# A decoder trunk on eight cores: the depthwise convolution as dense matmuls over four time phases, fewer expert weights cast ahead, token numbers scattered and rows gathered

## What is computed

```
u = xn @ w_pw1 + b_pw1                      # 1024 -> 2048
u = a * sigmoid(g)                          # a, g: halves of u
u = depthwise causal conv, width 31, over positions, + b_dw
u = silu(layer_norm(u, ln_g, ln_b)) @ w_pw2 + b_pw2
...
for e in range(16):                         # 2 nonzero weights per token
    y += combine[:, e] * ((silu(xf @ w_gate[e]) * (xf @ w_up[e])) @ w_down[e])
```

## Time and profile before

| what | us |
|---|---|
| median of 3 runs (2652.67 to 2663.49) | 2657.18 |
| the profiled execution | 2669.73 |
| its span, slowest core (core 2; the others from 2623.5) | 2668.7 |
| PE busy (share of the span) | 1926.4 (72%) |
| DVE, ACT, POOL busy | 882.5, 826.5, 391.1 |
| casts and other POOL-queue DMAs, share of 16 engines | 44.3% |
| SP-queue DMAs, share of 16 engines | 25.4% |

### The profile page before, as it was taken

The page is one execution under the profiler, slowest core; times in us unless marked ns, Lnnn a source line. Parts: engine busy times, 40 slices in busy tenths (PEclk is TensorE's granted clock), DMA queues, the critical chain, the costliest instruction groups (busy, mean ns, idle before and its releaser), DMA issues.

```text
span 2668.7 us, 35704 instructions; the slowest of 8 cores (2623.5 to 2668.7 us)
## 1 busy us (share of the span) xinstructions
PE 1926.4 (72%) x11760; PEld 1058.9 (40%) x11760; DVE 882.5 (33%) x1838; ACT 826.5 (31%) x1322; POOL 391.1 (15%) x469
## 2 busy tenths in 40 slices
PE   4999993770439998256777877777993389995557
PEld 1344440220125555122245655555631155553223
DVE  2321102440433332244443333333234423321433
ACT  2411115310112222133545555555511122221333
POOL 0010003201120001332300000010102300012243
PEclk9999995785669999566878999989996689997577
DMA  9999999999039998722235677788741169997333
GB/s 234 186 130 155 135 141 142 129 144 180 32 116 305 322 316 291 175 78 71 33 33 82 99 101 107 107 96 114 104 165 40 75 213 317 326 322 198 125 130 119
DMA packets 126134, 412.93 MB, mean 155 GB/s; under 512 B 34912, under 2 KB 34912, under 8 KB 101360
## 3 DMA queue, kind: packets, MB, share of 16 engines
q0 software_dynamic: 64544, 189.35, 44.3%
q1 hardware_dynamic: 60816, 220.07, 25.4%
q10 hardware_dynamic: 576, 1.05, 0.2%
HBM read 428.58 MB, written 205.78 MB: 238 GB/s over the span
## 4 chain that ended last, share of the span: by engine, by line
PE 63%; DVE 10%; DMA 9%; issue 7%; ACT 6%; another core or an unknown queue 2%; POOL 1%; DVEq 0%; ACTq 0%; SPq 0%; POOLq 0%
PE ps L256 59%; PE ps L260 5%; DMA xt<-xsd 3%; DMA gb<-ysd,slots 2%; ACT sq L273 2%; DMA h<-xT 2%; DMA ring<-w 1%; DVE gb L294 1%; DVE xnb L294 1%; ACT pt L273 1%; DVE q L294 1%; ACT rt L273 1%; DMA xsd<-xrow,slots 1%; ACT rstd L273 1%
## 5 line engine op out<-in xcount | busy, mean ns | idle before, releaser
L256 PE MATMUL ps<-xTT,ring 128*128 128x384 bf16 (+1 forms) x2304 | 355.4, 315 | 2.4 <-DVE xTT L300 2.0
L256 PE MATMUL ps<-sq,ones_bf 128*128 128x512 bf16 x288 | 140.3, 502 | 230.1 <-ACT sq L273 228.0
L256 PEld LDWEIGHTS ps<-xTT,ring 128*128 128x128 bf16 x2304 | 215.6, 98 | 141.1 <-issue 6.0
L256 PE MATMUL ps<-glu,dg 128*128 128x512 bf16 x992 | 216.9, 381 | 6.2 <-DVE dg L276 6.2
L256 PE MATMUL ps<-xgD,wh 128*128 128x512 bf16 x512 | 150.8, 447 | 84.7 <-DVE q L294 56.0
L273 ACT ACTIVATE pt<-ps,cst_s 128x512 bf16<-128x512 f32 (+1 forms) x288 | 180.6, 658 | 89.4 <-PE ps L256 83.0
L260 PE MATMUL ps<-cst_s,gb 128*128 128x128 f32 x256 | 62.1, 424 | 191.8 <-DVE gb L294 177.9
L273 ACT ACTIVATE sq<-h 128x512 bf16<-128x512 f32 x192 | 113.3, 623 | 219.3 <-PE ps L256 147.2
L256 PE MATMUL ps<-ring,hdn 128*128 128x512 bf16 x800 | 180.9, 382 | 0.5 <-DVE hdn L276 0.4
L256 PEld LDWEIGHTS ps<-sq,ones_bf 128*128 128x128 bf16 x288 | 29.7, 103 | 376.9 <-issue 372.8
L256 PE MATMUL ps<-xgA,w 128*128 128x512 bf16 x768 | 172.3, 388 | 3.6 <-DVE h L294 3.6
(11 more groups left out here) (184 smaller groups left out, 2590.4 us busy)
## 6 DMA issues: line engine op xcount, KB each, us to landing
w<-w_moe POOLq DMA_DIRECT2D x96, 1024.0 KB
ring<-w SPq DMA_DIRECT2D x96, 1024.0 KB
ysd<-ysb SPq DMA_DIRECT2D x96, 512.0 KB
xt<-xsd SPq DMA_DIRECT2D x32, 768.0 KB
xsd<-zt SPq DMA_DIRECT2D x16, 1024.0 KB
ysd<-zt SPq DMA_DIRECT2D x9, 1024.0 KB
yT<-h SPq DMA_DIRECT2D x32, 256.0 KB
h<-xT SPq DMA_DIRECT2D x28, 256.0 KB
```

Source lines behind the costliest of these rows:

```text
L256: return self.op('pe', lambda e: e.matmul(out, lhsT=lhsT, rhs=rhs, start=start, stop=stop, **kw), ins=[lhsT, rhs], outs=[out], inc=inc)
```

## The change

Four things. (1) The convolution. Channels are taken in 32 groups of 32, and a partition becomes (time modulo 4, channel in the group), so that a column holds four neighbouring tokens. The 31 taps become 9 shifts v of dense 128x128 matrices (4 x 4 phases, diagonal in the channel), each applied to the 512 columns that hold all 2048 tokens: 32 x 9 = 288 matmuls. DVE builds 36 such matrices for 4 groups in one operation (`build`). The layout is reached through DRAM: the gated output `gp` (3 buffers) is written to `gpd` by 4 DMAs and read back into `gc` by one (`regroup`), on SP, in runs of 512 bfloat16, for each chunk of 128 channels; after normalisation and Silu each chunk goes back the same way (one write on SP, 4 reads, two on ACT's queue). The first pointwise matmul now runs chunk by chunk over all tokens, its weights in four buffers of one chunk, read in runs of 128 columns; the convolution of chunk c-2 follows that of chunk c, and the sums for the layer norm run in between over two fixed PSUM banks. (2) Of layer 0 only 9 experts are cast ahead (27 casts, one after each unit of `pw1` from the second chunk on). The others, 0, 1, 2, 5, 8, 11 and 14, are loaded from float32 into `ring` on POOL's queue, and the spare experts of layer 0 fetch float32 rows. (3) Rows of x are written once, by SP, to `xnd`; only the token numbers are scattered, 4 bytes each, to `idxd`; `xi` reads them back and `load_x` gathers the rows on POOL's queue, three indirect DMAs for an expert, in both layers. `back` gets 17 more small DVE operations for these addresses. (4) `xsd` and its zeroing are gone; the 19 zeroing DMAs of `ysd`, 512 KB each, are issued on SP in layer 0's `back`.

```diff
+NA = CAP // 128
+IX1 = 16 * CAP
+NIDX = IX1 + 16 * 128 + 128
+PRE0 = tuple(e for e in range(3, 16) if e not in (5, 8, 11, 14))
...
+def pack_conv(inp):
+    wdw = np.asarray(inp['conv_w_dw'][0], dtype=np.float32).reshape(31, 32, 32)
+    wsh = np.zeros((4, 32, 32, 9, 4), dtype=np.float32)
+    for i in range(4):
+        for v in range(9):
+            for j in range(4):
+                k = 4 * v + i - j - 2
+                if 0 <= k <= 30:
+                    wsh[i, :, :, v, j] = wdw[k].T
...
-                S.dma('act' if tt0 == 0 and c % 2 else 'sp', h[:, c, tt0 * TT:(tt0 + 1) * TT],
-                      xv[:, c, tt0 * TT:(tt0 + 1) * TT])
-        casts = [(l, e, j) for l in range(2) for e in range(NE) for j in range(3)]
+                x_tok = S.dma('act' if tt0 == 0 and c % 2 else 'sp', h[:, c, tt0 * TT:(tt0 + 1) * TT],
+                              xv[:, c, tt0 * TT:(tt0 + 1) * TT])
+            x_toks.append(x_tok)
+        casts = [(l, e, j) for l in range(2) for e in (range(NE) if l else PRE0) for j in range(3)]
...
+
+                load_w1(0)
+                load_w1(1)
+                S.dma('act', cva[:], cva_d)
+                S.wait_tok('pool', x_toks[2])
+                load_w1(2)
+                S.wait_tok('pool', x_toks[3])
+                load_w1(3)
+                S.memset('pool', gc[:, :, 0:8], 0.0)
+                S.copy('dve', blk[:], cva[:, NG * 36:NG * 36 + 128])
+                m32 = cva[:, NG * 36 + 128:NG * 36 + 256].rearrange("p (j c) -> p j c", c=32)
+                S.memset('dve', zi[:], 0)
+                S.dma('act', idxd.rearrange("(p a) o -> p (a o)", p=128), zi[:], outs=[("idx", 0, 1, 0, 100)])
+
+                def build(c):
+                    S.tt('dve', dg[:, c % 2], m32.unsqueeze(1).to_broadcast([128, 36, 4, 32]),
+                         cva[:, c * 144:(c + 1) * 144].rearrange("p (a j) -> p a j", j=4).unsqueeze(3).to_broadcast([128, 36, 4, 32]),
+                         ALU.mult)
+
+                P1, P2 = PS[6], PS[7]
+                ps_set[0] = list(range(6))
+                done = [0]
+
+                def pw1(c, tt):
+                    pa = next_ps()
+                    pg = next_ps()
+                    for k in range(NC8):
+                        S.mm(pa[:], w1[:, c % 4, 0, k, :], xn(k, tt * TT, TT), k == 0, k == NC8 - 1)
+                    for k in range(NC8):
+                        S.mm(pg[:], w1[:, c % 4, 1, k, :], xn(k, tt * TT, TT), k == 0, k == NC8 - 1)
+                    S.act(sg[:, tt % 2, :], pg[:], AF.Sigmoid, bias=P('b_pw1', 8 + c))
+                    S.stt(gp[:, c % 3, :, tt * 128:(tt + 1) * 128].rearrange("p i u -> p u i"),
+                          pa[:].rearrange("p (u i) -> p u i", i=4), P('b_pw1', c),
+                          sg[:, tt % 2, :].rearrange("p (u i) -> p u i", i=4), ALU.add, ALU.mult)
+                    if c > 0 and len(casts) > NE * 3:
+                        pump(1)
+
+                def regroup(c):
+                    for gg in range(4):
+                        S.dma('sp', gpd[4 * c + gg].rearrange("i c u -> c i u"), gp[32 * gg:32 * gg + 32, c % 3],
+                              outs=[("gpd", 0, 1, 4 * c + gg, 4 * c + gg + 1)])
+                    S.dma('sp', gc[:, 4 * c:4 * c + 4, 8:GW], gpd[4 * c:4 * c + 4].rearrange("g i c u -> (i c) g u"),
+                          ins=[("gpd", 0, 1, 4 * c, 4 * c + 4)])
+                    if c + 4 < NC8:
+                        load_w1(c + 4)
+
+                def stats(g):
+                    S.mm(P1[:], blk[:], gc[:, g, 8:GW], g == 0, g == NG - 1)
+                    S.mm(P2[:], blk[:], sq[:, g % 2, :], g == 0, g == NG - 1)
+
+                def conv(c):
+                    for gg in range(4):
+                        g = 4 * c + gg
+                        ps = next_ps()
+                        for v in range(9):
+                            S.mm(ps[:], dg[:, c % 2, gg * 9 + v].rearrange("p j c -> p (j c)"), gc[:, g, v:v + TT],
+                                 v == 0, v == 8)
+                        S.act(gc[:, g, 8:GW], ps[:], AF.Identity, bias=P('b_dwP', g))
+                        S.act(sq[:, g % 2, :], gc[:, g, 8:GW], AF.Square)
+                        if g:
+                            stats(g - 1)
+
+                for tt in range(NTT):
+                    rms_tile(tt, 'g_mix', 0, lambda k, t1=tt: xn(k, t1 * TT, TT))
+                    for c in range(2):
+                        pw1(c, tt)
...
+                build(0)
+                regroup(0)
+                regroup(1)
+                for c in range(2, NC8 + 2):
+                    if c < NC8:
+                        for tt in range(NTT):
+                            pw1(c, tt)
+                        regroup(c)
+                    if c - 1 < NC8:
+                        build(c - 1)
+                    conv(c - 2)
+                stats(NG - 1)
+                p2.close()
                 w2 = sb("w2", [128, NC8, D], BF16, pc)
                 w2v = w_pw2.rearrange("(c p) n -> p c n", p=128)
                 for c in range(NC8):
                     S.dma('pool', w2[:, c, :], w2v[:, c, :])
-
-                def cvb(c, tt):
-                    return xn(c, tt * TT, TT)
...
                 mean = sb("meanA", [128, TT], F32, pc)
-                m2 = sb("m2A", [128, TT], F32, pc)
...
+                for g in range(NG):
+                    v = gc[:, g, 8:GW]
+                    S.tt('dve' if g % 5 in (1, 3) else 'pool', t1[:, g % 3, :], v, mean[:], ALU.subtract)
+                    S.tt('dve', t2[:, g % 3, :], t1[:, g % 3, :], rstd[:], ALU.mult)
+                    S.act(v, t2[:, g % 3, :], AF.Silu, bias=P('ln_bP', g), scale=P('ln_gP', g))
+                    c, gg = g // 4, g % 4
+                    if gg == 3:
+                        S.dma('sp', gpd[4 * c:4 * c + 4].rearrange("g i c u -> (i c) g u"), gc[:, 4 * c:4 * c + 4, 8:GW],
+                              outs=[("gpd", 0, 1, 4 * c, 4 * c + 4)])
+                        for q in range(4):
+                            S.dma('sp' if q % 2 else 'act', xg[0][32 * q:32 * q + 32, c, :].rearrange("p (i u) -> p i u", i=4),
+                                  gpd[4 * c + q].rearrange("i c u -> c i u"),
+                                  ins=[("gpd", 0, 1, 4 * c + q, 4 * c + q + 1)])
...
                 def load_w(e):
                     for j in range(3):
-                        S.dma('sp', ring[:, e % NBR, j * NIN:(j + 1) * NIN], w16[l][e, :, j * NIN:(j + 1) * NIN],
-                              ins=[("w16", 0, 1, (l * NE + e) * 3 + j, (l * NE + e) * 3 + j + 1)])
+                        if l or e in PRE0:
+                            S.dma('sp', ring[:, e % NBR, j * NIN:(j + 1) * NIN], w16[l][e, :, j * NIN:(j + 1) * NIN],
+                                  ins=[("w16", 0, 1, (l * NE + e) * 3 + j, (l * NE + e) * 3 + j + 1)])
+                        else:
+                            S.dma('pool', ring[:, e % NBR, j * NIN:(j + 1) * NIN].rearrange("p (a n) -> p a n", n=2048),
+                                  w_moe[l, e, :, j * NIN:(j + 1) * NIN].rearrange("p (a n) -> p a n", n=2048))
 
...
+                    S.copy('dve', pf[:], sf[:])
...
                     S.tt('dve', ov2[:], ov2[:], ok2[:], ALU.mult)
@@ -794,6 +885,24 @@
                     S.ts('dve', sf[:], sf[:], dump[:], ALU.add, 0.0, ALU.max)
...
+                    S.ts('dve', isl[:, tt % 2], ri[:], float(NIDX - 1), ALU.min)
+                    zero(5)
...
-                            S.dma('pool', xsd, xrow[:, i % 3, :], out_idx=slots[:, i, k:k + 1], ins=[("xsdz", 0, 1, 0, 100)],
-                                  outs=[("xsd", 0, 1, 2 * i + k, 2 * i + k + 1)])
+                            S.dma('pool', idxd, tokid[:, i:i + 1], out_idx=isl[:, tt % 2, i4, k:k + 1],
+                                  ins=[("idx", 0, 1, 50, 51)], outs=[("idx", 0, 1, 2 * i + k, 2 * i + k + 1)])
...
+                S.dma('sp', xi[:], idxd[0:IX1, :].rearrange("(p a) o -> p (a o)", p=128), ins=[("idx", 0, 1, 0, 51)])
...
+                for q in range(NSP):
+                    S.dma('pool', xs[:, q:q + 1], idxd, in_idx=ov0[:, 0, q:q + 1], ins=[("idx", 0, 1, 0, 51)])
...
                 def load_x(e):
-                    if e < NE:
-                        S.dma('sp', xt[:, e % 2, 0:CAP // 128], xsd[e * CAP:(e + 1) * CAP, :].rearrange("(a p) d -> p a d", p=128),
-                              ins=[("xsd", 0, 1, 0, 64)])
-                    else:
-                        S.dma('pool', xt[:, e % 2, 0, :], xsd, in_idx=ov0[:, 0, e - NE:e - NE + 1],
-                              ins=[("xsd", 0, 1, 0, 64)])
+                    for a in range(tiles_of[e]):
+                        S.dma('pool', xt[:, e % 2, a, :], xnd,
+                              in_idx=xi[:, e * NA + a:e * NA + a + 1] if e < NE else xs[:, e - NE:e - NE + 1],
+                              ins=[("xnd", 0, 1, 0, 16)])
```

183 lines of the change are left out of this document (91 added, 92 removed).

## The result

The changed kernel takes **2804.69 us** (median of 4 runs, 2768.11 to 2883.61), the kernel before 2659.66 beside it (2652.67 to 2663.49): ratio **1.0478**, 95% interval 1.0375 to 1.0581. Forecast were 2668, and at most 2725. The profiled execution is the run of 2768.11 us.

What follows compares the result with a forecast made beforehand. TensorE's 217 us and the casts' transfer time bound the first 780 us; in the experts both TensorE and DMA are full. Experts' start -41, layer 0's experts +45, layer 1 and the rest +6: +10, so 2668 us median, range 2575 to 2725.

Steps and rivals of the forecast that it cites:

- Casts and regroups alternate one for one: Convolution: each SP packet pays for one cast packet, so a regroup's 69 packets cost 7.7 casts, 73 us.
- what TensorE saves in the convolution is waited for: Convolution: the 154 us that TensorE saves are waited for; its end at 412 us, where before it was 400.
- Normalisation: Phase A after the convolution: 8.0 us per channel, 76 us in all against 86 before.
- The hole in the routing: Layer 0's routing: with no cast left ahead of the scatters on POOL, the 57 us stall goes.
- Layer 1's routing: Routing of layer 1: +14 us, from more small DVE operations and the added hops and POOL issues.
- Rival (a): Convolution: regroups aren't held by casts, pw2 ends at 476, 78 us less, 2590 us in all; chance 0.35.
- step 1: Front of phase A: first two channels take about 23 us, four times, from 21 us: 113; w1 loads let SP pass cheaply.
- step 2: Convolution's end: DMA sum 377, 393 with 2.4 at the start and about 14 idle, 19 more for hops and conv(7): 412 us.
- step 3: Experts: gathers of x in their own queue -5 us in layer 0; x out of SP's queue -8 in layer 1.
- step 4: Layer 0's experts: float32 loads 6.1 us against 3.3, twelve add +34 (to +75); spare experts' float32 rows +16.
- Routing of layer 0: Layer 0's routing: 57 us stall gone, +14 added; nobody waits for the scatters behind nine float32 loads before xi.
- rival (b): Experts: float32 loads cost more, above about 0.9 us per packet, and gathers come late: +50, 2718 us; chance 0.20.

Runs made afterwards that it cites:

- conv_direct: Kernel before with the new phase A (constants through SP), no casts in layer 0, all its experts loaded from float32, rows of x scattered as before: 2615.68 us profiled, no ratio.
- b_direct3: Kernel before with layer 0's experts 0 to 2 loaded directly from float32, not cast, and its spare experts' rows gathered from float32: ratio 0.9849.
- gp_plain: Changed kernel with the gated output written to gp in order, not spread over the four phases: ratio 1.0409 to the kernel before.
- front_fix: Changed kernel with the constants' load and idxd's zeroing on SP's queue and the block matrix copied after the first two channels: ratio 1.0298 to the kernel before.
- nocast: Changed kernel with no expert of layer 0 cast ahead, all 16 loaded from float32: ratio 1.0157 to the kernel before.
- b_gather: Kernel before with token numbers scattered and x gathered on POOL's queue, xsd and its zeroing gone, old phase A and all 48 casts kept: ratio 1.0142.
- x_plain_pool: Changed kernel with x of the 16 experts read by one plain DMA per expert on POOL's queue, in both layers: ratio 1.0243 to the kernel before.

## Why the prediction was wrong, point by point

**Right.** Casts and regroups alternate one for one, later channels stall 16 to 46 us each, and what TensorE saves in the convolution is waited for: 141 us, forecast 154, though 46 of them in the first channel, where none was forecast. TensorE alone would end it at 274: conv_direct ends there. Normalisation 71 us (forecast 76), pw2 58 (66). The hole in the routing goes (b_direct3). Layer 1's routing +15 (+14). Phases C and D unchanged. Rival (a), regroups that aren't held, fell.

**Wrong, step 1: the order at the front.** "About 23 us, four times, from 21 us: 113" ends the first two channels; 64 matmuls of the third stand ahead of the first convolution matmul, which puts it near 127. With no cast and neither of ScalarE's waits it starts at 130 (conv_direct); that this is so near is in part luck, since ScalarE starts 10 us earlier there than the forecast's 21, and DVE's spread write of 2.50 us, forecast as 0.75, costs some 10 (gp_plain). Two terms that the forecast put at nothing make the rest: ScalarE's two queue waits 26 (200 - 174, front_fix), and the casts 43 (200 - 157, nocast). 130 + 26 + 43 = 199, measured 200. For ScalarE the step costed the instructions but not the DMAs issued ahead of them on its own queue, against the forecast's own rule that every queue counts. For the casts it had said "Up to c=3 the new w1 loads of 130 short packets let SP packets pass cheaply". Where they stood side by side they did (153 to 156 us), but the loads were over by 166 us, and channel 0 waited until 203 for its read, by then one for one behind casts.

**Wrong, step 2: "DMA sum 377, idle about 14".** The sum was no bound, because the engines weren't kept at work. All of 0 to 447 us in the kernel after, columns as above:

```profile
0.00:447.00 447.00, 223.72 (x858) 88.47 (x876) 141.12 (x94) 94.56 (x139) 33.24 (x56) 0.78 0.80 118
```

0.80 of 447 us is 358 us of transfer, less than the 377; 89 us are idle, where 2.4, 14 and 19 were forecast. From 60 to 140 us alone, with a share of 0.14 to 0.31, 61 are. Casts are pumped by the pace of TensorE's channels, and only the second channel's pump in that stretch, one in some 23 us. The end, 447 against 412, is this idle time less what the sum had too much; the last regroup was the last thing late, as forecast. How much of it an earlier front gives back was tried: 15 us at the end for 26 at the start (front_fix).

**Wrong, step 3: "gathers of x in their own queue no longer stand behind ring loads: -5", and -8 in layer 1.** They cost: +35 in layer 0 and +22 in layer 1 beside the old phase A (b_gather); in the changed kernel layer 1 has +11. The step weighed the place in the queue and took the transfer as unchanged, though the earlier trace rows had a price only for gathers of longer rows. This is the largest error. x_plain_pool shows it by itself: 26 us less in layer 0, 7 or more in layer 1, and the queue is the same.

**Wrong in size, step 4: float32 loads.** 6.1 us each forecast, 6.7 measured; but an expert so loaded adds 8.6 to 9.7 us, where 3 x (6.1 - 3.3) = 8.4 was forecast: near. The spare experts' rows added some 27, forecast 16. The whole of +88 splits as 35 (gathers) + 27 (spare rows) and the rest, 26, for four direct experts, forecast 34; the three overlap, so they are no exact sum.

**Routing of layer 0** was forecast 43 us shorter and is 23 shorter: from 580 to 783 us the DMA share is 0.53 and not 0.29, the nine float32 loads in front of the scatters. The forecast had said that nobody waits for them; that this is the missing 20 us was not tried by itself. With the old scatters and nine such loads the routing takes 195 us in conv_direct and 178 in b_direct3.

So rival (b) had the right place and sign and named a smaller cause: the loads stayed under its 0.9 us per packet (6.7 x 16 / 128 = 0.84; the forecast counts eight packets per engine here and nine for the cast's 1.06), and gathers, spare rows and front made the difference, 113 us by the stages and 127 by the ratio.

## What to carry to other kernels

A saving of an engine counts only as far as its inputs are not in line with a queue that takes turns with casts of 8 KB: price each small transfer at one large packet of the other queue, count how many hops it has, and ask whether the casts are worth more than they hold up (here 15 us of phase A against 9 us of experts, for each expert cast). Before summing transfer times, find the stretch in which the issuing code is itself waiting and the DMA share is low. And where a change turns a plain load into a gather, price the gathered row from a row of that size, or bound it from both sides, and list the DMAs that each compute engine issues ahead of its first instruction.

## What the runs showed of the hardware that was not expected

- A gather of 2 KB rows took 3.2 to 7.7 us per MB inside one stage (b_gather) and 4.3 in layer 1 of the kernel after, a plain load of the same rows 3.2.
- DVE wrote 128x512 bf16 with neighbours 1 KB apart in 2.50 us, in order in 0.75. The Trainium skill, "SBUF — State Buffer", section "Door 1: The DMA port swizzle (why `[64,N]` ≈ `[32,N]`)", says that a line of SBUF is 16 bytes and that each access that crosses to another line pays a penalty; the trace agrees in direction, and no run tried a distance between.
- One for one holds for 1 KB packets against casts of 8 KB (143 to 144, and 146 to 147), and nearly against packets of 256 bytes (492 to 528 from 153 to 156 us). A count over 10 us can mislead: from 160 to 170 us it is 361 to 1944, but in 157 to 161 SP's queue passed nothing at all.
- In the convolution without casts TensorE's granted clock is 1.00, the level of 2.4 GHz (conv_direct, 130 to 274 us); with the waits of 20 to 50 us it is 0.77.
